# One more 16-bit product of 32 columns ahead of each group of eight gate products

## The reference, cut to what matters

```python
def peer_ffn(h, w_q, keys, u_tab, v_tab):
    ...
    q = (ht @ w_q).reshape(t, PEER_HEADS, 2, PEER_HALF)
    sc = jnp.einsum('thid,hikd->thik', q, keys).astype(jnp.float32)
    top_s, top_i = lax.top_k(sc, PEER_TOPK)
    ...
    experts = i1 * N_KEYS + i2
    gates = jax.nn.softmax(best_s, axis=-1).astype(h.dtype)
    ...
        act = jnp.einsum('thkd,td->thk', u_tab[eb], hb)
        coef = gb * jax.nn.gelu(act, approximate=False)
        return jnp.einsum('thk,thkd->td', coef, v_tab[eb])
```

## Time and profile before

| What | Value |
|---|---|
| median of three executions | 2833.22 us |
| profiled execution, its own time | 2834.17 us |
| its span, first to last instruction | 2832.4 us |
| mean granted clock of TensorE | 0.999 |
| DMA | 855.06 MB, mean 302 GB/s |

### The profile page before, as it was taken

The page is one execution under the profiler, slowest core; times in us unless marked ns, Lnnn a source line. Parts: engine busy times, 40 slices in busy tenths (PEclk is TensorE's granted clock), DMA queues, the critical chain, the costliest instruction groups (busy, mean ns, idle before and its releaser), DMA issues.

```text
span 2832.4 us, 49104 instructions
## 1 busy us (share of the span) xinstructions
PE 2785.6 (98%) x17864; PEld 2590.7 (91%) x17864; DVE 2493.2 (88%) x5020; ACT 1387.9 (49%) x2321; POOL 952.5 (34%) x773
## 2 busy tenths in 40 slices
PE   7999999999999999999999999999999999999998
PEld 4767789999999999999988788999999999999998
DVE  4667789999999799999987679999999979999998
ACT  3345225477777433333353532445777753333333
POOL 1000018833335244444400000694333434434342
PEclk9999999999999999999999999999999999999999
DMA  7434648999999899999932122699999999999996
GB/s 276 181 119 178 246 157 305 352 337 399 389 382 348 335 387 384 393 390 392 395 119 75 60 74 83 223 345 334 391 386 393 362 335 365 383 386 382 396 387 251
DMA packets 257144, 855.06 MB, mean 302 GB/s; under 512 B 26080, under 2 KB 59104, under 8 KB 250336
## 3 DMA queue, kind: packets, MB, share of 16 engines
q1 hardware_dynamic: 149280, 442.23, 42.1%
q0 software_dynamic: 98496, 381.73, 35.7%
q10 hardware_dynamic: 9216, 29.36, 2.6%
HBM read 777.06 MB, written 76.15 MB: 301 GB/s over the span
## 4 chain that ended last, share of the span: by engine, by line
PE 66%; DVE 19%; DMA 7%; issue 4%; ACT 3%; POOL 1%; SPq 0%; DVEq 0%; ACTq 0%; POOLq 0%
PE banks L1099 32%; PE banks L1636 8%; PE banks L1633 8%; PE banks L1640 8%; DMA w_raw<-wst 5%; PE banks L1597 3%; DVE w_lo L1680 2%; DVE stages L2180 2%; DVE vacc L2192 2%; PE banks L1434 2%; PE banks L1171 1%; ACT w_hi L811 1%; DVE pick L2300 1%; DVE pick L2304 1%; DMA pj<-adaw 1%
## 5 line engine op out<-in xcount | busy, mean ns | idle before, releaser
L811 ACT ACTIVATE w_hi<-w_raw 128x1024 fp32r<-128x1024 f32 x596 | 628.4, 1055 | 632.2 <-PE banks L1099 322.6
L1680 DVE TENSOR_TENSOR w_lo<-w_raw,w_hi 128x1024 fp32r<-128x1024 f32 x522 | 637.8, 1222 | 236.5 <-ACT w_hi L811 192.1
L769 POOL DMA_INDIRECT ring<-v,gidx x320 | 394.1, 1232 | 610.6 <-DVE vacc L2192 520.4
L1099 PE MATMUL banks<-hH,w_hi 128*128 128x352 f32 (+1 forms) x2528 | 513.4, 345 | 2.0 <-ACT act_out L1025 2.0
L1099 PE MATMUL banks<-hH,w_lo 128*128 128x352 f32 (+1 forms) x2528 | 492.2, 336 | 3.2 <-POOL w_lo L756 1.6
L1099 PE MATMUL banks<-hL,w_hi 128*128 128x352 f32 (+1 forms) x2528 | 490.9, 336 | 0.0
L1099 PEld LDWEIGHTS banks<-hH,w_hi 128*128 128x128 f32 x2528 | 415.7, 188 | 39.5 <-issue 11.0
L1099 PEld LDWEIGHTS banks<-hH,w_lo 128*128 128x128 f32 x2528 | 427.0, 188 | 24.9 <-POOL w_lo L756 3.7
L1099 PEld LDWEIGHTS banks<-hL,w_hi 128*128 128x128 f32 x2528 | 427.6, 188 | 19.0
L769 POOL DMA_INDIRECT ring<-u,gidx x244 | 281.8, 1155 | 455.0 <-DVE gact L2180 444.3
L2192 DVE SCALAR_TENSOR_TENSOR vacc<-ring,gcoef,vacc 128x1024 f32<-128x1024 f32 x316 | 404.2, 1279 | 7.1
(11 more groups left out here) (354 smaller groups left out, 3895.9 us busy)
## 6 DMA issues: line engine op xcount, KB each, us to landing
w_raw<-wst SPq DMA_DIRECT2D x596, 512.0 KB, 6.6
activations<-act_out SPq DMA_DIRECT2D x124, 352.0 KB, 8.0
act_in<-activations SPq DMA_DIRECT2D x62, 704.0 KB, 7.3
gate_matrices<-stages ACTq DMA_DIRECT2D x64, 448.0 KB, 7.8
gates<-gate_matrices SPq DMA_DIRECT2D x64, 448.0 KB, 8.9
ada_buf<-adaw POOLq DMA_DIRECT2D x24, 1024.0 KB, 6.9
nrm<-adaw POOLq DMA_DIRECT2D x8, 1024.0 KB, 5.2
pj<-adaw POOLq DMA_DIRECT2D x7, 1024.0 KB, 7.1
```

The lines of the kernel that those rows point to most:

```text
L769: pool.indirect_dma_start(out=gather_slot(l, k), out_offset=None, in_=rows[:, :], in_offset=bass.IndirectOffsetOnAxis(ap=gidx[:, k % UG:k ...
L811: nc.scalar.activation(w_hi[g % 2][:, :, :].rearrange("p a b -> p (a b)"), w_raw[:, g % RAWS, :], ACT.Copy).then_inc(s_wh, 1)
L1099: last = mm(bank[s][:, 0:t.stop - t.start], a[s][:, k, :], b[:, k, t], start=(k == 0 and a is w_hi and b is hH), stop=(k == KT - 1 and a i ...
L1680: v.tensor_tensor(w_lo[g % 2][:, :, :].rearrange("p a b -> p (a b)"), w_raw[:, g % RAWS, :], w_hi[g % 2][:, :, :].rearrange("p a b -> p (a ...
```

## The change

`gate_quad` issues one more product ahead of the eight. Its stationary operand is that of the first of the eight, and its moving operand is the first 32 columns of the same one-hot rows. It writes 32 of the columns that the first of the eight then overwrites with `start=True`. Nobody reads its result, it signals nothing, and it waits for nothing more than the first did.

```diff
                 def gate_quad(u):
 
                     oh = oneh[u % OH_SLOTS]
+                    mm(by_expert(u)[:, 0:32, 0], oh[:, 2, 0, :], oh[:, 1, 0, 0:32].bitcast(BF16), start=True, stop=True)
                     for t in range(QUAD):
                         for part in range(2):
                             last = mm(by_expert(u)[:, :, t], oh[:, 2 + part, t, :], oh[:, 1, t, :].bitcast(BF16),
                                       start=(part == 0), stop=(part == 1))
                     last.then_inc(s_gm, 1)
```

## The result

The changed kernel takes 2848.37 us, the median of six executions (2847.90 to 2849.93), against 2833.52 us of the kernel before (six executions, 2832.99 to 2837.76). The ratio is 1.005, with a 95% interval of 1.0037 to 1.0063: slower by 0.5%, 14.9 us, where 4.5 us were forecast.

The account below looks back on a forecast made before the run. PE (TensorE) was taken as the bound, also in the gate stretches; 176 x 28 ns = 4.9 us, less 0.4 us of waits, gave 4.5 us on 2833.22: 2837.7 us, range for 8 in 10 2829.5 to 2844.5.

Parts of the forecast that it names:

- 176 new products at 28 ns: In gate_quad on PE, one added product for each of 176 groups, 28 ns each, 4.9 us in all.
- The neighbour in 32 bits: Two 32-bit products of 32 columns at the layer's end, the second starting some 30 ns after the first.
- half of the 56: Half of the 56 ns that a full 128-column gate product takes on PE, giving the 28 ns price.
- 0.4 us given back by waits: In the gate stretches of both layers, a later PE waits less for other engines, 0.4 us less.
- Rival 1: At the gate groups, 32 columns cannot hide the next load: 56 ns each, 9.5 us, 2842.7 us; chance 0.20.
- the 18.8 and 9.4 us: Estimated total costs of the new gate products if each load takes 107 ns or 53 ns, by the Trainium skill.
- Rival 3: At the gate groups, the new product shares the next one's load: 14 ns each, 2.5 us or less; chance 0.06.
- Rival 2: The shift changes u-tile speeds: all quick, 2824.4 us (all or most, chance 0.14), or all slow, 2851.0 us (0.05).
- the sign to which I gave 0.05: All u tiles on PE turn slow: 4.5 + 13.3 = 17.8 us more, 2851.0 us; chance 0.05.
- a double group shifts like a single one: Between u tiles, a double group's eight more products shift nothing: after 3.87 us, a group of 16, then 4.04 again.
- the cheap price: New gate product priced by columns alone, 14 ns each, 2.5 us; 2.1 us more in the range.
- a third of the slow tiles: A rhythm change in 26 slow u tiles, 0.17 us each, 4.4 us less, used for the range's lower end.

## Why the prediction was wrong, point by point

- **PE is the bound, and a nanosecond on it is one of the whole:** right. The intervals account for 13.5 of 14.0 us.
- **176 new products at 28 ns, 4.9 us:** close, 25 ns. The groups grew by 4.4 us in 154 intervals. The neighbour in 32 bits with 30 ns, and half of the 56, were a fair guide, but columns alone do not set the price: 32 and 48 columns cost the same. The Trainium skill's floor of about 25 ns in "TensorE: Matmul & The Clock Gate", section "Wait — 56ns, not 53.3ns?", is what the groups of 430 and 455 ns show, and its estimate of 4.4 us was the better one. 64 columns cost 29 ns, 128 cost 56.
- **0.4 us given back by waits:** the right sign, about 1 us.
- **Rival 1, the load shows:** it did not. A product of 32 columns adds 25 ns including the load behind it, and one of 128 adds 56. Neither the 9.5 us of the rival nor the 18.8 and 9.4 us worked out beside it were paid.
- **Rival 3, a shared load:** it did not happen either. The trace has 176 loads more, and a product adds 25 ns, not 14.
- **Rival 2, the rhythm:** this is what happened, with the sign to which I gave 0.05. Its own mark came too: quick tiles are rare, and the two gate stretches grew by 5.6 and 7.9 us. The step that failed is the sentence that a shift "would make the speed stick over single groups, and then the ten double groups in each layer, with two new products, would turn it over: again about half of the tiles are slow, and nothing but the 28 ns is left". I took the two speeds as symmetrical, each handed on or turned, so that half of the tiles must be slow in either case. They are not. For most lengths one of them wins: the tiles fall into it sooner or later and are back in it soon after a double group, slow with 32, 48, 66 and 82 columns, quick with 64, 80 and 128. The sum for all slow was +13.3 us for 78 tiles; 60 tiles changed, for 10.4 us.
- **That a double group shifts like a single one:** right for the kernel before, and confirmed by the run with one product of 64 columns for each tile. But two new products in a double group shift twice, which is why 17 of the 20 tiles behind double groups are slow with 64 columns.
- **The range:** its lower end does not follow from its terms: the cheap price (+2.1 us) and a third of the slow tiles turned quick (-4.4 us) make 2830.9 us, not 2829.5. At the upper end the rival reached to 2851.0, and I ended the range at 2844.5, trusting the symmetry for which the trace of before had no row.

## What to carry to other kernels

When a stream of equal products shows two speeds that change where another kind of work is put in between, the length of that work is a setting, and its cost cannot be had from its own duration. Before such an insertion is taken or thrown away, try it at some lengths over a period of 16 cycles: here 32 columns cost 0.5% and 64 columns, once for each tile, gained 0.2%. Count the tiles at each speed, since the busy share of the engine does not show them.

## What the runs showed of the hardware

- 32-bit products of 352 columns follow each other at 158 ns (in the mean of 155 to 162) or at 167 ns, with all operands and code the same, by when the row of them begins. Steady intervals of tile and group are multiples of 16 cycles of 2.4 GHz (6.7 ns): 10448, 10464, 10512, 10880, 10896, 10912. Products longer by 16 columns (66 and 82, 72 and 88, 64 and 80), and by 64 (64 and 128), do alike.
- What lies behind the 16 cycles is open. No run here varied the 32-bit products themselves, their addresses or the transfers beside them. Very small differences go with large ones: behind a slow tile the group takes 461.6 ns with 66 columns, and the next tile is slow (113 of 114 times); with 72 columns it takes 462.4 ns there, and the next tile is quick (all 55 times). Whether these 0.8 ns are the cause or a consequence of the rhythm, no run shows.
- A 16-bit product of 32 or 48 columns that loads its own 128 x 128 stationary operand adds 25 ns to PE's line, one of 64 adds 29, of 80 36, of 128 56.
